# Two encoder layers in float32 on one core: where the second layer's modulation weights are worked off

## The reference, cut to what matters

```python
c_act = jax.nn.silu(c)
for l in range(DEPTH):                                   # DEPTH = 2, SEQ = 256, D_MODEL = 1024
    mod = (c_act @ w_mod[l] + b_mod[l])[:, None, :]      # 1 x 6144 per layer
    sh1, sc1, g1, sh2, sc2, g2 = jnp.split(mod, 6, axis=-1)
    h = rmsnorm(x, norm1_g[l]) * (1.0 + sc1) + sh1
    proj = h @ w_in[l]
    ...                                                  # attention, convolution, state space; three gates
    x = x + g1 * (mixed @ w_out[l])
    h2 = rmsnorm(x, norm2_g[l]) * (1.0 + sc2) + sh2
    gu = h2 @ w_ffn_in[l]
    f_gate, f_up = jnp.split(gu, 2, axis=-1)
    x = x + g2 * ((jax.nn.silu(f_gate) * f_up) @ w_ffn_out[l])
return rmsnorm(x, final_norm_g)
```

## Time and profile before

| what | value |
|---|---|
| median of 3 runs | 1089.7 us (1088.8 to 1093.1) |
| the profiled execution's own time | 1087.98 us |
| its span (first to last instruction) | 1086.2 us |
| TensorE, VectorE, ScalarE busy | 978.6, 676.5, 451.0 us |
| mean granted TensorE clock | 0.952 of full speed |
| bytes loaded | 191.5 MB, 177 GB/s over the span |
| mixing, first layer (`su0` to `fg0`) | 53.6 to 369.5 us |
| FFN, first layer | 369.5 to 597.1 us |
| mixing, second layer | 604.5 to 882.8 us |
| FFN, second layer | 882.8 to 1077.6 us |

### The profile page before, as it was taken

One profiled execution on the slowest core, in us unless ns is written; L12 is line 12 of the kernel. 1 busy time (PEld: TensorE's weight loads), 2 busy tenths in 40 slices (PEclk: granted clock), 3 DMA queues, 4 the chain that ended last, 5 costly groups with the idle time before them and its releaser, 6 DMA issues.

```text
span 1086.2 us, 19518 instructions
## 1 busy us (share of the span) xinstructions
PE 978.6 (90%) x8615; PEld 909.3 (84%) x8615; DVE 676.5 (62%) x908; ACT 451.0 (42%) x498; POOL 8.7 (1%) x14
## 2 busy tenths in 40 slices
PE   3687999879898799999999899996999979999998
PEld 1487888768788698989999899886889979999998
DVE  0498587988655558447544574897886645445444
ACT  1455316631453533453433522564235444334343
POOL 3000000000000000000000000000000000000000
PEclk9688899989999899999999899999899979999999
DMA  9852434547678445675675824444557525555531
GB/s 301 227 165 78 161 105 171 191 155 210 212 254 228 167 152 172 235 257 167 228 258 202 225 87 157 156 155 155 150 179 245 165 84 186 194 175 178 192 116 40
DMA packets 138997, 193.79 MB, mean 178 GB/s; under 512 B 25354, under 2 KB 117906, under 8 KB 132768
## 3 DMA queue, kind: packets, MB, share of 16 engines
q1 hardware_dynamic: 138272, 191.58, 53.9%
q0 software_dynamic: 368, 0.83, 0.4%
q10 hardware_dynamic: 272, 0.13, 0.0%
HBM read 191.48 MB, written 1.05 MB: 177 GB/s over the span
## 4 chain that ended last, share of the span: by engine, by line
PE 63%; DVE 23%; ACT 5%; DMA 4%; issue 3%; ACTq 0%; DVEq 0%; SPq 0%
PE bank L468 18%; PE bank L469 17%; PE bank L470 17%; DVE wlo L1180 8%; DVE yc L1460 5%; PE bank L501 2%; PE bank L527 2%; DMA raw<-in_w_mod 2%; ACT whi L889 2%; PE bank L548 1%; PE bank L571 1%; DMA raw<-in_w_attn_o 1%; DMA raw<-in_w_in 1%; PE bank L559 1%; PE bank L666 1%
## 5 line engine op out<-in xcount | busy, mean ns | idle before, releaser
L1180 DVE TENSOR_TENSOR wlo<-raw,whi 128x2048 fp32r<-128x2048 f32 x132 | 302.2, 2291 | 277.3 <-PE bank L470 213.1
L468 PE MATMUL bank<-hhi,whi 128*128 128x256 f32 x1504 | 443.2, 295 | 26.0 <-DVE tmp L1501 10.8
L469 PE MATMUL bank<-hlo,whi 128*128 128x256 f32 x1504 | 435.2, 289 | 0.0
L470 PE MATMUL bank<-hhi,wlo 128*128 128x256 f32 x1504 | 434.6, 289 | 0.0
L468 PEld LDWEIGHTS bank<-hhi,whi 128*128 128x128 f32 x1504 | 298.8, 199 | 43.4 <-issue 21.9
L889 ACT ACTIVATE whi<-raw 128x2048 fp32r<-128x2048 f32 x132 | 251.8, 1908 | 160.1 <-DMA raw<-in_w_in 67.0
L469 PEld LDWEIGHTS bank<-hlo,whi 128*128 128x128 f32 x1504 | 298.9, 199 | 0.1
L470 PEld LDWEIGHTS bank<-hhi,wlo 128*128 128x128 f32 x1504 | 298.4, 198 | 0.0
L468 PE MATMUL bank<-bhi,whi 128*128 128x256 f32 x608 | 177.0, 291 | 14.7 <-DVE tmp L1501 8.3
L469 PE MATMUL bank<-blo,whi 128*128 128x256 f32 x608 | 173.7, 286 | 0.0
L470 PE MATMUL bank<-bhi,wlo 128*128 128x256 f32 x608 | 173.5, 285 | 0.0
(11 more groups left out here) (237 smaller groups left out, 697.6 us busy)
## 6 DMA issues: line engine op xcount, KB each, us to landing
raw<-in_w_mod SPq DMA_DIRECT2D x48, 1024.0 KB, 7.3
raw<-in_w_ffn_in SPq DMA_DIRECT2D x44, 1024.0 KB, 5.1
raw<-in_w_in SPq DMA_DIRECT2D x38, 1024.0 KB, 6.3
raw<-in_w_ffn_out SPq DMA_DIRECT2D x22, 1024.0 KB, 5.0
raw<-in_w_out SPq DMA_DIRECT2D x8, 1024.0 KB, 7.0
raw<-in_w_in SPq DMA_DIRECT2D x16, 256.0 KB, 5.1
raw<-in_ssm_glu_b SPq DMA_DIRECT2D x4, 1024.0 KB, 6.0
raw<-in_ssm_glu_a SPq DMA_DIRECT2D x4, 1024.0 KB, 4.9
```

The source lines that it names most:

```text
L468: mm(o, w_hi, a_hi, start=start, stop=False, skip_group_check=True)
L469: mm(o, w_hi, a_lo, start=False, stop=False, skip_group_check=True)
L470: return mm(o, w_lo, a_hi, start=False, stop=stop, skip_group_check=True)
L1180: V.tensor_tensor(wlo[mi % N_LO][:, :], raw[SLOT[("main", *divmod(mi, NB))]][:, :], whi[mi % N_HI][:, :].bitcast(F32), ALU.subtract).then_ ...
```

## The change

The second layer's modulation blocks are placed elsewhere; nothing else is. Before, the first layer's FFN (with the two ahead of `fg0` of the first layer) held the whole first third and six blocks of the second, the last two of the second stood ahead of the second layer's `su0`, and the third third stood in the second layer's mixing, one every three blocks. After, the FFN holds the first third alone, one every four blocks; the first two blocks of the second third stand ahead of `su0`, the other six at the places that the first layer's mixing uses, and the third third too is at the first layer's places.

```diff
-MOD_AT = {0: {5 + 3 * (n // 2) + n % 2: (1, n) for n in range(DK)} | {18 + 3 * (n // 2) + n % 2: (2, n) for n in range(DK)},
-          1: {6 + 3 * n: (2, n) for n in range(DK)}}
+NORM_MODS = 2
+MOD_AT = {0: {5 + 3 * (n // 2) + n % 2: (1, n) for n in range(DK)} | {18 + 3 * (n // 2) + n % 2: (2, n) for n in range(DK)}}
+MOD_AT[1] = {i: m for i, m in MOD_AT[0].items() if m[0] == 2 or m[1] >= NORM_MODS}
...
-NEXT_THIRDS = [(ng, k) for ng in range(2) for k in range(DK)]
-NEXT_MOD_AT = {PREP_AT + 2 + 2 * n + 2 * (n >= DK - NORM_MODS): NEXT_THIRDS[NORM_MODS + n] for n in range(2 * DK - 2 * NORM_MODS)}
+NEXT_MOD_AT = {PREP_AT + 2 + 4 * n: (0, NORM_MODS + n) for n in range(DK - NORM_MODS)}
...
     if l and i == 0:
-        found = [(l, *m) for m in NEXT_THIRDS[-NORM_MODS:]]
+        found = [(l, 1, n) for n in range(NORM_MODS)]
...
-            found = [(l + 1, *m) for m in NEXT_THIRDS[:NORM_MODS]]
+            found = [(l + 1, 0, n) for n in range(NORM_MODS)]
```

More of the change, by code:

```diff
@@ L129 @@
 PREP_AT = AT[("fg", 1)]
-NORM_MODS = 2
-NEXT_THIRDS = [(ng, k) for ng in range(2) for k in range(DK)]
-NEXT_MOD_AT = {PREP_AT + 2 + 2 * n + 2 * (n >= DK - NORM_MODS): NEXT_THIRDS[NORM_MODS + n] for n in range(2 * DK - 2 * NORM_MODS)}
+NEXT_MOD_AT = {PREP_AT + 2 + 4 * n: (0, NORM_MODS + n) for n in range(DK - NORM_MODS)}
 B_ROUNDS, ROUNDS = 2 * STEPS, 2 * STEPS + 2
```

## The result

The changed kernel takes 1098.53 us (median of 6 runs, 1096.28 to 1101.7); the kernel before took 1091.67 us beside it (6 runs, 1088.8 to 1093.1). The ratio is 1.007, 95% interval 1.0048 to 1.0091: slower by 0.7%, 7.6 us on the 1089.7 us from which I had forecast 1093.9. (The two medians are 6.9 us apart.

The account below looks back on a forecast made before the run. TensorE was taken to hold 63% of the chain, VectorE 23%, with the FFNs TensorE-bound and the mixings partly idle. Terms: -5.0 - 0.8 + 0 + 10.0 = +4.2 us, forecast 1093.9 us on the median, range 1088 to 1098.5.

Parts of the forecast that it names:

- The stretch from `gs0` to `ga0`: Second layer's mixing: two blocks added ahead of 11 and 14 vanish in TensorE's waits; 0, bounds -1.7 to +2.0 us.
- the 0 for the block that goes ahead of 6 and comes ahead of 8: Second layer's start: one block removed, one added, both before the same rotary step, so 0 us.
- the attention comes late too: Rival, `gs1` to `glb1`: late loads and roundings hold up the exponentials; +5.4 us on the forecast, 1099.3 us, chance 0.16.
- `ga1` to `wo1`, +10.0: Second layer: four added blocks and the first layer's load list, so its 91.30 us instead of 81.30; +10.0 us.
- the same four marks: Signs, `ga1` to `wo1`: `ao0` wait about 3 us, ScalarE wait about 6, load between `in_w_attn_o` halves, `cp1` wait near 1.5.
- The first FFN, -5.0: First layer's FFN: twelve modulation blocks become six, five net savings of 1.0 us; -5.0 us, `fu2` wait growing.
- The start of the second layer, -0.8: Column step ahead of `q0` moves into idle time ahead of `ga0`; -0.8 us.
- After `wo1`, nothing: Second layer after `wo1`: no modulation block among the loads, before or after, so nothing changes; FFN stays 194.8 us.
- TensorE time only: Rival: second mixing's added blocks and column step cost TensorE time, but loads come in time; 1088.5 us, chance 0.16.
- All hidden: Rival: the second mixing's idle time hides all six added blocks, leaving only -5.8 us; 1083.9 us, chance 0.08.

Follow-up runs that it names:

- TensorE's time alone: Kernel before, plus matmuls of six modulation blocks on data already in SBUF, at the change's places in the second layer, without loads: 1090.36 us, 1.0004.
- The run with the loads later from index 8 on: Changed kernel, with the second layer's modulation loads for index 8 or later put two places later in SyncE's list: 1085.24 us, 0.997.
- the later loads: Changed kernel, with every modulation load of the second layer put two places later in SyncE's list: 1095.72 us, 1.0037.
- the third third alone: Kernel before, with only the second layer's third third at the change's places, the second third still in the FFN: 1101.08 us, 1.0098.

## Why the prediction was wrong

The forecast, +4.2 us, was too low: by 3.4 us against the ratio's +7.6, by 2.7 against the 6.9 us between the medians. The result, 1098.53 us, is 4.6 above the 1093.9, because the kernel before, too, measured 2.0 us more in six runs than the 1089.7 from which I counted. That it lies 0.03 us above the upper end of the range, and not inside, is that shift; but that it lies so far up is no accident.

**The step that failed: "The stretch from `gs0` to `ga0`", "I take 0".** It cost 3.5 us, or 4.1 us counted from `ca1` to `ga1`. I took the price of two added blocks for their matmuls' time, and that is indeed 0 there (TensorE's time alone: 87.4 us). What I left out is that a moved modulation block also takes a `raw` buffer which only TensorE gives back. I had read SyncE's list for `ga1` to `wo1` and worked out the late load there in full; the same reading of `ca1` to `ga0` would have shown the loads of `gs1` and `gla0` behind modulation blocks as well. The run with the loads later from index 8 on has the same blocks and takes 87.2 us: shown. With it fell the 0 for the block that goes ahead of 6 and comes ahead of 8: put back at 6, it gives the stretch 1.7 us. 3.6 of the 4.1 us lie between `ca1` and `ga0` and are the loads'. The other 0.5, between `ga0` and `ga1`, go with the clock. Before and after:

```profile
762.70:771.10 8.40, 8.38 (x56) 7.46 (x56) 7.17 (x13) 0.86 (x2) 0.00 (x0) 0.80 0.01 2
763.60:772.50 8.90, 8.90 (x57) 7.93 (x57) 7.34 (x14) 0.60 (x1) 0.00 (x0) 0.74 0.00 0
```

TensorE was granted 0.80 of its clock there and then 0.74; 8.40 x 0.80 and 8.90 x 0.74 are both 6.6 to 6.7 us of full clock, the same work. With the loads in time the stretch is 9.1 us at 0.73, so this part does not come back with them.

The rival "the attention comes late too" named this mechanism, the rounding ahead of the exponentials, and priced it at +5.4; its chance was 0.16. Its reason was half right: `gla0`'s transfer was the first to go out of its group and took 7.2 us from issue to landing; what made it late is that it was issued at 711.06. My argument against it, VectorE's backlog, fell: VectorE itself waits in the changed kernel, 1.44 us for ScalarE's split of the state-space input (L1017) and 1.24 us for the exponentials ahead of `glb0`.

**`ga1` to `wo1`, +10.0: right in its sum (+10.4) and mis-sized in its parts.** By the same four marks the first layer was a good stand-in: a wait of 3.23 in `ao0` ended by the sigmoid, 6.58 on ScalarE, the modulation block between the halves of `in_w_attn_o`, 1.55 in `cp1`, all as named. But the four blocks and the moved column step are 2.8 us and not 4.9 (the blocks alone 1.6 and not 4.0), and the two late loads with the half clock behind them 7.6 us and not 4.7 (91.7 against the 84.1 us with the same blocks and the loads in time). Two errors of opposite sign nearly cancelled; that the sum came out to 0.4 us is owed to copying a measured stretch, and in part to luck, since that stretch itself took 90.5 to 94.7 us from profile to profile. That the first layer's own figure already held a loss of 7.5 us, to be had back by one line, I did not see.

**The first FFN, -5.0: right in kind, -4.2 measured.** The wait at `fu2` grew by exactly the removed block. TensorE is busy 5.2 us less (214.68 against 219.88), where six blocks net would be 6.0. The clock can account for the rest: in `fo3` stands a wait of 2.02 us, and behind it the changed kernel's row over 4 us is

```profile
471.00:475.00 4.00, 3.90 (x20) 3.93 (x21) 3.09 (x3) 1.57 (x2) 0.00 (x0) 0.57 0.21 57
```

at a granted clock of 0.57, which by itself costs up to 1.7 us. The kernel before has the same wait there (2.01 us) and a granted clock of 1.00 behind it. Of the six profiles with this FFN and the old first-layer list five read 223.1 to 223.4 us and one 224.9, so the shortfall is no accident of one run.

**The start of the second layer, -0.8:** measured -0.7, right. **After `wo1`, nothing:** right, apart from the clock.

**The rival "TensorE time only"** (1088.5 us) is what the kernel would be if the loads cost nothing; the run with later loads from index 8 on comes nearest to it: 1088.5 would be 0.999, the upper end of its interval. **"All hidden"** fell: even with the loads in time `ga1` to `wo1` is 2.8 us longer, 1.6 of it the four blocks' matmuls.

**The range** ended at 1098.5 because I added all upper bounds of the terms that I had. A missing mechanism is not in such a sum; the bound of the failed term, +2.0, was that of TensorE's time alone. From the ratio the change costs 5.2 to 9.9 us; on 1089.7 us that is 1094.9 to 1099.6, most of it inside my range.

## What to carry to other kernels

When work is moved whose data comes through a shared ring of buffers, look at who empties each buffer and when, and read the in-order list of loads at every place that the work is moved to, not only at the one that already stalls. A load whose consumer needs no preparation belongs as late in such a list as its use allows, behind those that two more engines must still convert: here that order was worth 0.8 to 1.0%, and the placement of the work itself nothing that these runs can tell. It was not so everywhere: at the start of the second layer the later loads cost 5.9 us. And a stretch elsewhere in the program that already runs the new order told the price well, but with its own faults in it: ask what is wrong there before copying it.

## What the hardware showed that I had not expected

- At 348 to 350 GB/s of weight loads TensorE stood 1.95 us with nothing to wait for but its own issue, among 256 small matmuls, and ran at a granted clock of 0.50 over 10.2 us; `su0` to `cb0` was 5.9 us longer than in the changed kernel, which moves 213 GB/s at the same place and has no such wait. Whether the transfers are the cause is not shown; that the later modulation loads cost time at this place is.
- Waits of about the same length are followed by half clock in one kernel and not in another: behind the 2.52 us wait in `wo0` of the first layer the kernel before kept its clock, and behind the same wait of the same code the changed kernel had 7 us at 0.51. That alone is up to 3.4 us between two profiles, as much as one term of a sum like mine. The ledger of a single profile should be held against the ratio of medians.
- A wait that becomes longer need not be a delay: with the third third alone the wait for `kT` was 3.06 us, as long as in the changed kernel, because TensorE came to `gs0` 1.2 us earlier (8.2 instead of 9.4 us behind `ca1`). The length of the stretch decides.
